# Regrouping the experts of a two-layer mixture: 22 blocks with strips of 32 columns in place of 25, empty slots skipped, results scattered to token order, five weight buffers

## What is computed

```python
p_g = softmax(x @ wr_g + br_g); g_sel = argmax(p_g); w_g = max(p_g)
sel = (x @ wr_e + br_e) of the 8 experts of group g_sel
top_v, top_i = top_k(sel, 2)
gate = w_g * softmax(top_v)
...
y = (silu(x @ w_gate[e]) * (x @ w_up[e])) @ w_down[e]
out[token] = gate0 * y0 + gate1 * y1
```

## Time and profile before

| | |
|---|---|
| time, median of 3 runs | 2150.88 us (2149.66 to 2151.88) |
| span of the profiled execution, first to last instruction | 2143.7 us (its own time is not given; the span is 7.2 us under the median) |
| PE busy | 2004.4 us, 94% |
| DVE, ACT, POOL busy | 812.5, 532.2, 188.4 us |
| layer 0: first weight load, first PE transposes of expert rows, last down matmuls | 785.41, 820.90, 1111.77 us |
| layer 1: the same | 1766.21, 1800.07, 2091.03 us |
| first gather of expert rows, layer 0 and layer 1 | 815.63, 1794.5 us |
| weight loads | 64 of 2048 KB and 64 of 1024 KB, 192 MiB in all |
| read and written in HBM | 285.5 MB, 47.3 MB |

### The profile page before, as it was taken

The page is one execution under the profiler, slowest core; times in us unless marked ns, Lnnn a source line. Parts: engine busy times, 40 slices in busy tenths (PEclk is TensorE's granted clock), DMA queues, the critical chain, the costliest instruction groups (busy, mean ns, idle before and its releaser), DMA issues. The chain is left out here.

```text
span 2143.7 us, 28374 instructions
## 1 busy us (share of the span) xinstructions
PE 2004.4 (94%) x11085; PEld 1161.1 (54%) x11085; DVE 812.5 (38%) x1889; ACT 532.2 (25%) x1294; POOL 188.4 (9%) x283
## 2 busy tenths in 40 slices
PE   8999999889997988999998999999999988999990
PEld 4545554488543964444445657777675554444440
DVE  1114555867353463111115524444352134111115
ACT  1003233433111321111133433333331110111112
POOL 0000002001162211000002000000000001000003
PEclk9999999989998989999999999999999988999995
DMA  3500100020021147999985000000020018999987
GB/s 138 226 28 6 40 20 4 1 82 4 2 90 53 41 175 302 403 423 426 424 335 204 23 0 1 1 1 1 1 80 23 30 46 331 387 425 424 425 354 265
DMA packets 51389, 334.68 MB, mean 156 GB/s; under 512 B 6832, under 2 KB 7152, under 8 KB 33200
## 3 DMA queue, kind: packets, MB, share of 16 engines
q1 hardware_dynamic: 39376, 289.63, 33.1%
q0 software_dynamic: 11872, 43.13, 5.5%
HBM read 285.48 MB, written 47.25 MB: 155 GB/s over the span
## 5 line engine op out<-in xcount | busy, mean ns | idle before, releaser
L221 PE MATMUL psum<-arena 128*128 128x512 f32 (+12 forms) x9694 | 1863.2, 385 | 79.6 <-issue 29.0
L221 PEld LDWEIGHTS psum<-arena 128*128 128x128 f32 (+3 forms) x9694 | 1010.5, 168 | 877.7 <-issue 783.6
L2193 DVE TENSOR_TENSOR arena<-psum,arena 128x256 f32<-128x256 f32 x50 | 21.2, 425 | 423.1 <-ACT arena L2243 423.1
L1541 ACT ACTIVATE arena<-arena 128x1024 f32<-128x1024 f32 x43 | 45.4, 1056 | 249.7 <-DVE arena L2940 105.6
L2279 POOL DMA_INDIRECT arena<-xn_rows,arena x50 | 47.2, 944 | 657.4 <-PE psum L2154 443.4
L2243 ACT ACTIVATE arena<-psum 128x256 f32<-128x256 f32 x50 | 19.2, 385 | 322.0 <-PE psum L221 322.0
L2853 ACT ACTIVATE arena<-psum,arena 128x1024 f32<-128x1024 f32 (+8 forms) x72 | 50.2, 699 | 188.6 <-DVE arena L2889 188.6
L1242 ACT ACTIVATE arena<-psum 128x256 f32<-128x256 f32 (+3 forms) x128 | 44.0, 356 | 102.3 <-PE psum L221 91.4
L2236 ACT ACTIVATE arena<-psum 128x512 f32<-128x512 f32 x50 | 29.9, 597 | 148.1 <-PE psum L221 148.1
L2882 DVE TENSOR_TENSOR psum<-psum,arena 128x128 f32<-128x128 f32 (+2 forms) x72 | 20.3, 283 | 103.5 <-PE psum L221 103.2
L2387 DVE SCALAR_TENSOR_TENSOR arena<-arena 128x1024 f32<-128x1024 f32 (+1 forms) x34 | 43.5, 1281 | 30.7 <-DMA arena<-expert_rows,arena 29.4
(11 more groups left out here) (303 smaller groups left out, 1306.5 us busy)
## 6 DMA issues: line engine op xcount, KB each, us to landing
arena<-in_w_exp SPq DMA_DIRECT2D x64, 2048.0 KB, 18.4
arena<-in_w_exp SPq DMA_DIRECT2D x64, 1024.0 KB, 17.7
expert_rows<-arena SPq DMA_DIRECT2D x66, 512.0 KB, 14.9
arena<-in_x SPq DMA_DIRECT2D x16, 512.0 KB, 4.6
xn_rows<-arena SPq DMA_DIRECT2D x16, 512.0 KB, 2.6
arena<-in_w_out SPq DMA_DIRECT2D x8, 512.0 KB, 8.1
arena<-in_w_o SPq DMA_DIRECT2D x1, 4096.0 KB, 12.3
out<-arena SPq DMA_DIRECT2D x8, 512.0 KB, 5.3
```

Of the source, the lines that this page charges most:

```text
L221: return e.matmul(out, lhsT, rhs, start=start, stop=stop, skip_group_check=True)
L1541: return e.activation(junk, h[:, s, :], ACT.Square, accum_out=sq_sum[:, s:s + 1])
```

## The change

1. **22 blocks.** Six blocks hold one expert (places 4 to 9 in the sorted order), seven hold two (places 18 to 31), and nine are built of four strips of 32 rows: three strips of one expert and one strip of a fourth expert, which is spread over three blocks (`TRIPLES`). So twelve experts (places 0 to 3 and 10 to 17) have 96 rows each. Every strip is a matmul of its own with 32 stationary columns. Experts 0 to 3 now have the first places.
2. **Empty slots.** The table carries a number outside the tensor for an empty slot; gather and scatter skip such rows (`bounds_check`).
3. **Results in token order.** The gate is multiplied in when a block's result leaves PSUM, and POOL scatters the rows to place 2 * token + choice of `expert_rows` (in place of SP's store). The combine becomes one plain DMA of 8 KB a token on SP's queue and two additions. The zero fill at the start is gone. The gates are carried through the same index matmul, whose moving operand has 76 columns in place of 41.
4. **Five weight buffers.** A table assigns them (`BUFFER`, `AFTER`). SP loads five experts at once when the routing is done.
5. Tiles are laid out anew; the three latent weights are loaded from POOL's queue.

The core of the diff:

```diff
-N_BIG = 18
-N_PAIRS = (NE - N_BIG) // 2
-NM = N_BIG + N_PAIRS
+N_FIRST, LEAD = 4, 1 << 16
+assert LEAD > NE * (L + 1)
+NM = 22
 NBLK = NM + NOV
-
-PAIR_AT = (3, 6, 9, 12, 16, 19, 22)
-SEQ, RANKS = [], []
-for _i in range(NM):
-    _pairs = sum(_at < _i for _at in PAIR_AT)
-    if _i in PAIR_AT:
-        SEQ.append(N_BIG + _pairs)
-        RANKS.append((N_BIG + 2 * _pairs, N_BIG + 2 * _pairs + 1))
-    else:
-        SEQ.append(_i - _pairs)
-        RANKS.append((_i - _pairs,))
-LOADED = [(_rank, _i) for _i in range(NM) for _rank in RANKS[_i]]
-
-N_FIRST, LEAD = 3, 1 << 16
-assert LEAD > NE * (L + 1) and LOADED[:N_FIRST] == [(_n, _n) for _n in range(N_FIRST)]
-SLOTS = NBLK * P
+N_BUF = 5
+EMPTY, SPLIT = 1 << 14, 1 << 13
+
+
+TRIPLES = [((0, 1, 2), 3), ((10, 11, 12), 16), ((13, 14, 15), 17)]
+CAP, BASE, STRIPS = [0] * NE, [0] * NE, [[] for _ in range(NM)]
+for _ranks, _split in TRIPLES:
+    _at = (0, 9, 12)[TRIPLES.index((_ranks, _split))]
+    for _i, _r in enumerate(_ranks):
+        CAP[_r], BASE[_r] = 96, P * (_at + _i)
+        STRIPS[_at + _i] = [(_r, 32 * _q, 32) for _q in range(3)] + [(_split, 96, 32)]
+    CAP[_split], BASE[_split] = 96, SPLIT + P * _at
+for _i in range(6):
+    CAP[4 + _i], BASE[4 + _i], STRIPS[3 + _i] = P, P * (3 + _i), [(4 + _i, 0, P)]
+for _i in range(14):
+    CAP[18 + _i], BASE[18 + _i] = 64, P * 15 + 64 * _i
+    STRIPS[15 + _i // 2].append((18 + _i, 64 * (_i % 2), 64))
+
+
+SEQ = [0, 1, 2, 3, 15, 4, 16, 9, 10, 11, 5, 17, 6, 18, 12, 13, 14, 19, 7, 20, 21, 8]
+assert sorted(SEQ) == list(range(NM))
+LOADED = []
+for _b in SEQ:
+    LOADED += [_r for _r in sorted({_strip[0] for _strip in STRIPS[_b]}) if _r not in LOADED]
+assert sorted(LOADED) == list(range(NE)) and sorted(LOADED[:N_FIRST]) == list(range(N_FIRST))
+USED = [[_i for _i, _b in enumerate(SEQ) if _r in {_strip[0] for _strip in STRIPS[_b]}] for _r in LOADED]
+
+
+BUFFER, AFTER, _free = [], [], [(-1, _i) for _i in range(N_BUF)]
+for _n in range(NE):
+    _free.sort()
+    _at, _buf = _free.pop(0)
+    assert _at < USED[_n][0]
+    AFTER.append(_at)
+    BUFFER.append(_buf)
+    _free.append((USED[_n][-1], _buf))
+FREED, TOP_BUFFER = min(_free)
...
+            after()
+            for j, what in enumerate(("rank_cap", "rank_base")):
+                e.tensor_scalar(y.by_rank[0:NE, j, :], y.place[0:NE], col("rank_no", 0, NE), col(what, 0, NE), ALU.is_equal,
+                                ALU.mult).then_inc(*y.placed.up())
...
+            dest = y.dest.rearrange("p a b -> p (a b)").bitcast(I32)
+            for u, (shift, mask) in enumerate(((0, P - 1), (7, 63), (5, 3), (13, 1))):
+                out = y.parts_i[:, u, :].bitcast(I32)
+                if shift:
+                    e.tensor_scalar(out, dest, shift, mask, ALU.logical_shift_right, ALU.bitwise_and).then_inc(*V.up())
+                else:
+                    e.tensor_scalar(out, dest, mask, None, ALU.bitwise_and).then_inc(*V.up())
+            after()
+            e.tensor_copy(y.parts, y.parts_i.bitcast(I32)).then_inc(*V.up())
+            after()
+            row, blk, strip, split = (y.parts[:, u, :] for u in range(4))
+            e.tensor_tensor(y.moved, strip, split, ALU.mult).then_inc(*V.up())
+            e.scalar_tensor_tensor(out=row, in0=split, scalar=96.0, in1=row, op0=ALU.mult, op1=ALU.add).then_inc(*V.up())
+            after()
+            e.scalar_tensor_tensor(out=row, in0=y.moved, scalar=-32.0, in1=row, op0=ALU.mult, op1=ALU.add).then_inc(*V.up())
+            e.tensor_tensor(blk, blk, y.moved, ALU.add).then_inc(*V.up())
+            after()
+            rows, blks = (t.rearrange("p (a b) -> p a b", b=2) for t in (row, blk))
             for j in range(2):
-                after()
-                e.tensor_tensor(y.blk1[j], bc_mid(y.io48, ns), y.blkf[:, :, j:j + 1].to_broadcast([P, ns, NBLK]), ALU.is_equal).then_inc(*V.up())
-                after()
-                e.tensor_tensor(y.blk1[j], y.blk1[j], bc_last(y.tokf, NBLK), ALU.mult).then_inc(*V.up())
+                e.tensor_tensor(y.eq[j], bc_mid(y.io48, ns), blks[:, :, j:j + 1].to_broadcast([P, ns, NBLK]), ALU.is_equal).then_inc(*V.up())
+            after()
+            for j in range(2):
+                e.tensor_tensor(y.blk1[j][:, :, 0:NBLK], y.eq[j], bc_last(y.code[j], NBLK), ALU.mult).then_inc(*V.up())
+                e.tensor_tensor(y.blk1[j][:, :, NBLK:], y.eq[j], y.gates[:, :, j:j + 1].to_broadcast([P, ns, NBLK]), ALU.mult).then_inc(*V.up())
+            after()
+            for m in y.m_xs[-3:]:
+                e.wait_ge(*m)
             for s in range(ns):
                 for j in range(2):
-                    e.tensor_scalar(y.row1[2 * s + j], y.io128, y.rowf[:, s, j:j + 1], None, ALU.is_equal).then_inc(*y.hot.up())
-
-            for r in range(1, NE // 8):
-                before = y.key if r == 1 else y.left
-                e.wait_ge(*y.sorted.at(r))
-                e.scalar_tensor_tensor(out=y.left, in0=before, scalar=y.k8[:, 7:8], in1=before, op0=ALU.is_lt, op1=ALU.mult).then_inc(*V.up())
-                after()
-                eight(r, y.left)
+                    e.tensor_scalar(y.row1[2 * s + j], y.io128, rows[:, s, j:j + 1], None, ALU.is_equal).then_inc(*y.hot.up())
+
+            for r in range(2, NE // 8):
+                next_eight(r)
...
-            e.tensor_copy(idx.bitcast(I32), y.tb.bank["idx"][:, 0:NBLK]).then_inc(*y.tb.drain("idx", "V"))
+            e.tensor_scalar(to_row.bitcast(I32), y.tb.bank["idx"][:, 0:NBLK], float(EMPTY), None, ALU.add).then_inc(*y.indexed.up())
+            e.wait_ge(*y.indexed.last())
+            e.tensor_scalar(from_row.bitcast(I32), to_row.bitcast(I32), 1, None, ALU.logical_shift_right).then_inc(*y.indexed.up())
+            e.tensor_copy(gate_of, y.tb.bank["idx"][:, NBLK:2 * NBLK]).then_inc(*y.tb.drain("idx", "V"))
...
-            keep_busy(e, banks[7], 11)
+            keep_busy(e, banks[7], 3)
+            e.wait_ge(*y.placed.at(2))
+            mm(e, y.tb.bank["caps"][:, 0:2 * NE], ones[0:NE, :], y.by_rank[0:NE].rearrange("p a b -> p (a b)"), True,
+               True).then_inc(*y.tb.fill("caps"))
+            keep_busy(e, banks[7], 8)
...
         def sp_gate_up(e, y, n):
-            if n >= 4:
-                e.wait_ge(*y.ex.full(("gu", LOADED[n - 4][1])))
-            e.dma_start(y.gu[n % 4], weights_of(e, y, n)[:, 0:WG]).then_inc(d_gu[n % 4].sem, 16)
+            if AFTER[n] >= 0:
+                e.wait_ge(*y.ex.full(("gu", AFTER[n])))
+            e.dma_start(y.gu[n], weights_of(e, y, n)[:, 0:WG]).then_inc(d_gu[BUFFER[n]].sem, 16)
 
         def sp_down(e, y, n):
-            if n >= 4:
-                e.wait_ge(*y.ex.full(("y", LOADED[n - 4][1], 1)))
-            e.dma_start(y.dn[n % 4], weights_of(e, y, n)[:, WG:]).then_inc(d_dn[n % 4].sem, 16)
+            if AFTER[n] >= 0:
+                e.wait_ge(*y.ex.full(("y", AFTER[n], 1)))
+            e.dma_start(y.dn[n], weights_of(e, y, n)[:, WG:]).then_inc(d_dn[BUFFER[n]].sem, 16)
...
             wait_all(e, ring.free(key))
             for k in range(KD):
-                for rows, w in shares(ws):
+                for rows, w in shares:
                     m = mm(e, ring.bank[key][rows], xt[:, k, rows], gu_weights(w)[:, k, :], k == 0, k == KD - 1)
...
-                e.tensor_copy(y.y[b % 3][:, half_cols(0)], y.ex.bank[key]).then_inc(*y.ex.drain(key, "V"))
+                e.tensor_scalar(y.y[b % 3][:, half_cols(0)], y.ex.bank[key], gate_of[:, SEQ[b]:SEQ[b] + 1], None,
+                                ALU.mult).then_inc(*y.ex.drain(key, "V"))
...
         def gather(e, xe, block, sem):
             e.indirect_dma_start(out=xe, out_offset=None, in_=xn_dram[:, :],
-                                 in_offset=bass.IndirectOffsetOnAxis(idx.bitcast(I32)[:, block:block + 1], 0)).then_inc(sem, 16)
+                                 in_offset=bass.IndirectOffsetOnAxis(from_row.bitcast(I32)[:, block:block + 1], 0),
+                                 bounds_check=L - 1, oob_is_err=False).then_inc(sem, 16)
+
+        def scatter(e, rows, block, sem):
+            e.indirect_dma_start(out=y_dram[:, :], out_offset=bass.IndirectOffsetOnAxis(to_row.bitcast(I32)[:, block:block + 1], 0),
+                                 in_=rows, in_offset=None, bounds_check=2 * L - 1, oob_is_err=False).then_inc(sem, 16)
 
         def pool_experts(e, y):
-            e.wait_ge(*y.tb.empty("idx"))
+            e.wait_ge(*y.indexed.at(2))
             for p in range(y.ns - 3, y.ns):
                 e.wait_ge(*y.m_xs[p])
-            for b in range(NM):
-                if b >= 3:
-                    e.wait_ge(*y.ex.full(("x", b - 3, 1)))
-                gather(e, y.xe[b % 3], SEQ[b], d_xe[b % 3].sem)
-
-        def sp_store(e, y, b):
-            e.wait_ge(*y.ex.empty(("y", b, 0)))
-            e.wait_ge(*y.ex.empty(("y", b, 1)))
-            e.dma_start(y_dram[P * SEQ[b]:P * (SEQ[b] + 1), :], y.y[b % 3]).then_inc(d_y[b % 3].sem, 16)
...
```

(33 more changed lines are left out.)

319 lines of the change are left out of this document (171 added, 148 removed).

## The result

| | before | after |
|---|---|---|
| median of 4 runs, same chip | 2150.27 us (2142.1 to 2151.88) | 2118.93 us (2114.54 to 2122.15) |
| ratio, 95% interval | | 0.9861 (0.9837 to 0.9885) |
| profiled execution: span | 2143.7 us | 2120.4 us (its own time 2122.15) |
| layer 0: first weight load; first transposes; last down matmuls | 785.41; 820.90; 1111.77 us | 787.98; 828.38; 1099.79 us |
| layer 1: first transposes; last down matmuls | 1800.07; 2091.03 us | 1798.19; 2069.03 us |

Faster by 1.4%, 31.3 us between the medians, where 43.6 us were forecast (2107 us, range 2094 to 2135). The direction and the range hold; the size is 12 us short, and 2118.9 lies just beyond the 2100 to 2117 us that had the chance of 0.62. The profiled execution is the slowest of the four after, so trace against trace the difference is only 23.3 us.

A forecast was written before the change was run, and what follows sets the result against it. PE was taken to set the expert stages' time, with DMA nearly even; 2 x (-28.2 + 1.6 + 5.3) - 1 = -43.6 us against the median of 2150.88 gave 2107 us, range 2094 to 2135.

The forecast's parts named there:

- Blocks on PE: Expert stage: 12 fewer single blocks at 11.39 us, nine four-strip blocks at 12.05 us; -28.2 us a layer.
- the pair's 12.05: Period in us of a two-expert block in the earlier trace, taken as the cost of a four-strip block.
- the single's 11.39: Period in us of a one-expert block in the earlier trace, the lower bound for a four-strip block.
- The rivals of three or two overlapping strips: Strip matmuls on PE overlap only three at a time (2167 us, chance 0.09) or two (2293 us, chance 0.04).
- DMA waiting: Expert stage: PE waits for weight loads that need freed buffers; +1.6 us a layer, range 0 to 7.
- The bookkeeping: Estimate of PE's waits from keeping the list of loads at 425 GB/s, 360 in the first 60 us.
- DMA binds: Rival: skipped rows still cost time or scattered writes are slower, 10 us a layer reaches PE; 2127 us, chance 0.14.
- Table: Routing table before the first gather: longer DVE chain +1.6 us, other work +0.4; first gather starts 2.0 us later.
- First gather: Start of the expert stage: gather behind five queued loads lands in 8.2 us; with the table +5.3 us a layer.
- another 2: Upper case at the first gather: PE, out of keep-busy work, may fall to 1.2 GHz and lose 2 us more.
- Combine: Final: DVE's 16 additions become plain ones, 1.22 us each instead of 1.28; -1 us.
- Zero fill: Removing the 8.4 MB fill, which ran under PE's projections, was counted at nothing.

The follow-up runs named there:

- less to load: Kernel after with only the first half of each expert's down weights loaded: 2152.97 us, layer 1 routed otherwise; layer 0's stage took 258.1 us against 271.4.
- turned blocks: Kernel after with nine of 22 blocks sending slot p to partition 127 - p: 2107.38 us, ratio 0.9799; with empty slots moved too, 2125.71 us.
- nothing left out: Kernel after with every empty slot gathering and scattering a row of its own instead of being skipped: 2125.93 us, ratio 0.9904.
- the zero fill: Kernel after with the earlier kernel's 16 zero-fill stores and the waits for them put back: 2121.14 us, ratio 0.988.
- the warm start: Kernel after with ten more keep-busy matmuls behind the index matmuls, ahead of the first block: 2120.47 us, ratio 0.9881.
- the fifth expert later: Kernel after with the fifth expert's load held on SP until the first gather has landed: 2107.69 us, ratio 0.9821.

## Why the prediction held, and where it was off

- **Blocks on PE, -28.2 us a layer.** Right in kind and too small. PE's own work in the stage was 290.9 less 0.65 of waiting before, 290.2 us, and is 258.1 with less to load: -32.1. Solved for nine strip blocks this is 11.6 us each (the stage of layer 0 alone was measured so); I took the pair's 12.05, the nearer end was the single's 11.39. The rivals of three or two overlapping strips needed records of 0.15 us and more; they measured 0.109. The Trainium skill ("TensorE: Matmul & The Clock Gate", Part 3) gives 3.07x for four tiles of 32 rows; taken over to four strips of 32 columns it is not borne out here, where 0.109 us stand against 0.442 for the full width.
- **DMA waiting, +1.6 us a layer, 0 to 7.** This is the step that failed. Waits went from 0.65 to 8.5 and 8.2 us, and 1.4 us of slow clock came behind the long one: +9 and +9. The bookkeeping added up bytes and moved them at the mean rate. It took leaving out a row for 4 KB off the list, when it takes 4 KB off one of 16 lists, and mostly not off the longest. The sign that I gave for "DMA binds" (over 7 us a layer, the DMA at its ceiling) was met, and that rival's condition, skipped rows that still cost their time, was more than half true: 7 us of gain, where turned blocks give 18. That the time still fell within the range is in part luck: the strips gave 4 us a layer more than I had counted, against 7.5 more of waiting.
- **Table, +2.0 us.** The chain from cast to one-hot takes 4.29 us (805.67 to 809.96), +1.3 where I had +1.6. In this execution the destinations are ready 17.7 us after the first weight load, not 18.8 as before, so the first gather is issued only 0.4 us later (30.6 for 30.2). That is not the rule: in layer 1 it is issued 3.4 us later (31.6 for 28.2), and in six other runs with unturned blocks 2.5 to 2.9 us later in layer 0. The +2.0 lies between. The 76 columns cost nothing: 13.55 us for the 46 records, as foreseen.
- **First gather, +5.3 us a layer with the table.** +4.9 in layer 0 (40.4 for 35.5), 9.7 us to land where I had 8.2; issued 2 us later behind the same five loads it landed in 8.2 to 8.6 us in three other runs (nothing left out, the zero fill, the warm start). In layer 1 the transposes come 40.5 us after the keep-busy work begins, 33.8 before: +6.7, table included. The mechanism was right, and the run with the fifth expert later shows it alone. The fall of the clock stood in the range with "another 2" and should have stood in the sum: 2.9 us.
- **Combine, -1 us.** Behind layer 1's experts the rest of the span is 1.3 us shorter. From layer 0's last down matmuls to layer 1's first weight load it takes 3.4 us longer; 2.7 of them stand at the latents, whose matmuls run at the lower clock for longer than before. I had nothing there.
- **Zero fill, 0.** Right.
- **The sum.** Trace against trace: starts +4.9 and +6.7, stages -19.5 and -20.1 (290.9 to 271.4, 291.0 to 270.8), what lies between the two layers' experts +3.4 and the final -1.3 make -25.9. In the untouched code ahead of layer 0's experts, 2.6 us were lost, which I put to the spread of single executions (2114.5 to 2122.2) without having tested it. That leaves the 23.3 seen. Against the forecast the strips gave 4 us more a layer, the waits with their clock took 7.5 more, the cold start 2.9 more: 6.5 a layer, 13 us in both, where 12 are missing.

## What to carry to other kernels

In these traces a load is complete only when its fullest share is, 17.6 us after the first one where PE waited longest. When rows are skipped, count what is left on each of the 16 shares and not the bytes; put the empty slots at different partitions in different blocks, or skipping saves little (7 us here, where turned blocks made it 18). And before a small transfer that everything waits for, do not queue a large one that nobody needs yet: holding back one load of five gave 11 us.

When two resources are nearly even, the price of the tighter one is the estimate to distrust. A quick way to it is a run that takes load off it and one that puts load on: here the first, with 39 us less of DMA work in a layer, ended the waits and took 13 us off it, and the second, with 29 us more in two layers that already waited, added only 7. A list that sets the stage at its mean rate would have handed on most of the 29, and that pointed at the shares.

## What the hardware showed that I had not expected

- Four fp32 column strips of 32 overlap fully: 0.109 us for each record of 512 moving columns, against 0.222 for strips of 64 and 0.442 for 128 columns in the earlier trace rows.
- In the kernel after, a DMA share of 1.00 at 415 GB/s (1000 to 1020 us) hid a spread of 17 to 20 us between the shares of one load; before, 1.01 at 425 GB/s went with less than 5. The mean tells nothing of the fullest.
- 4.5 us of idle time were enough for a fall to 1.2 GHz in the work behind them (1.88 for 1.04 us, 9.17 for 7.07, granted clock 0.50); so were 5.3 us. Waits of 1.3 and 2.0 us left the matmuls behind them at 7.09; behind one of 2.23 us (fifth expert later) they took 8.69. The length of one wait does not settle it: in layer 1 of the run with less to load, idle times of 1.31 and 0.84 us with the eight transposes between them were followed by 8.77 us for 7.07.
- A gather of 128 slots behind five queued weight loads lands in 8.2 to 9.7 us, against 4.3 without the last of them. How to even out the 8 to 10 us of spread that are left with turned blocks was not tried.
